# Another order of the steps within a slot on VectorE and ScalarE, in the mixing stage of a diffusion layer

## What is computed

```
o_rw  = (o_fwd + o_bwd), group norm per head of 64 channels, * ln_w + ln_b, + bonus, * gate
o_gla = (o_fwd + o_bwd), RMS norm per head of 96 channels, * norm_w * silu(g)
o     = concatenate([o_lru, o_rw, o_gla]) @ w_out            # 1024 x 1024
x     = x + g1 * o
h     = rmsnorm(x, norm2_g) * (1 + sc2) + sh2
probs = softmax(h @ w_router)                                # 16 experts
```

## Time and profile before

| | |
|---|---|
| median of 3 executions | 3443.15 us (3442.53 to 3450.62) |
| profiled execution, its own time | 3448.97 us |
| profiled execution, span | 3447.2 us |
| TensorE busy | 3111.8 us, 90% of the span |
| VectorE busy | 2279.6 us, 66% |
| ScalarE busy | 1609.5 us, 47% |
| GpSimd busy | 878.8 us, 25% |
| mixing stage, from the start of the first `rw_centre` to that of the last `keep_probs` | 1728.08 to 2044.66 us |

### The profile page before, as it was taken

One profiled execution on the slowest core, in us unless ns is written; L12 is line 12 of the kernel. 1 busy time (PEld: TensorE's weight loads), 2 busy tenths in 40 slices (PEclk: granted clock), 3 DMA queues, 4 the chain that ended last, 5 costly groups with the idle time before them and its releaser, 6 DMA issues. The chain is left out here.

```text
span 3447.2 us, 90906 instructions
## 1 busy us (share of the span) xinstructions
PE 3111.8 (90%) x37105; PEld 2856.9 (83%) x37105; DVE 2279.6 (66%) x4490; ACT 1609.5 (47%) x2917; POOL 878.8 (25%) x1232
## 2 busy tenths in 40 slices
PE   7899989999689999999869961999999999999996
PEld 4887867767489999999857740999999999999996
DVE  5565549995478888888777758555555555555555
ACT  3313656665445545554456530444444444444454
POOL 0110000000066667676422201012111111111113
PEclk8999989999899999999989975999999999999998
DMA  6455336665644554444276632556656556556685
GB/s 203 139 163 170 94 88 203 201 198 152 186 122 108 131 151 111 110 109 109 56 209 186 177 125 76 165 186 196 208 186 195 186 185 194 185 184 190 206 286 187
DMA packets 583428, 561.43 MB, mean 163 GB/s; under 512 B 211550, under 2 KB 527262, under 8 KB 582138
## 3 DMA queue, kind: packets, MB, share of 16 engines
q1 hardware_dynamic: 546652, 446.02, 43.2%
q0 software_dynamic: 36016, 109.52, 10.8%
q10 hardware_dynamic: 432, 1.25, 0.1%
HBM read 418.33 MB, written 138.33 MB: 161 GB/s over the span
## 5 line engine op out<-in xcount | busy, mean ns | idle before, releaser
L3456 DVE TENSOR_TENSOR exp_wlo<-exp_raw,exp_whi 128x2048 fp32r<-128x2048 f32 x192 | 439.9, 2292 | 366.3 <-ACT exp_whi L3357 354.4
L3357 ACT CAST exp_whi<-exp_raw 128x2048 fp32r<-128x2048 f32 x189 | 360.0, 1905 | 76.8 <-DMA exp_raw<-in_w_up 74.2
L1042 PE MATMUL mix_acc<-proj_hThi,mix_wlo 128*128 128x448 f32 (+3 forms) x920 | 357.6, 389 | 14.4 <-DVE mix_wlo L1410 14.4
L1042 PE MATMUL mix_acc<-proj_hTlo,mix_whi 128*128 128x448 f32 (+3 forms) x920 | 335.6, 365 | 0.0
L1042 PE MATMUL mix_acc<-proj_hThi,mix_whi 128*128 128x448 f32 (+3 forms) x920 | 335.4, 365 | 0.0
L3286 PE MATMUL moe_o<-moe_hidhi,exp_wlo 128*128 128x272 f32 x1024 | 307.5, 300 | 2.6 <-DVE moe_hidlo L3570 2.6
L3286 PE MATMUL moe_g<-moe_xThi,exp_wlo 128*128 128x272 f32 x1024 | 300.1, 293 | 1.0 <-DVE moe_xTlo L3460 1.0
L3286 PE MATMUL moe_o<-moe_hidhi,exp_whi 128*128 128x272 f32 x1024 | 297.8, 291 | 0.0
L3286 PE MATMUL moe_g<-moe_xThi,exp_whi 128*128 128x272 f32 x1024 | 297.3, 290 | 0.0
L3286 PE MATMUL moe_u<-moe_xThi,exp_wlo 128*128 128x272 f32 x1024 | 296.7, 290 | 0.0
L3286 PE MATMUL moe_u<-moe_xThi,exp_whi 128*128 128x272 f32 x1024 | 296.4, 289 | 0.0
(11 more groups left out here) (395 smaller groups left out, 8539.5 us busy)
## 6 DMA issues: line engine op xcount, KB each, us to landing
exp_raw<-in_w_gate SPq DMA_DIRECT2D x64, 1024.0 KB, 5.0
exp_raw<-in_w_up SPq DMA_DIRECT2D x64, 1024.0 KB, 5.1
exp_raw<-in_w_down SPq DMA_DIRECT2D x64, 1024.0 KB, 6.7
scn_plain<-rec SPq DMA_DIRECT2D x68, 384.0 KB, 3.8
rec<-mix_arena SPq DMA_DIRECT2D x24, 896.0 KB, 4.4
proj<-mix_out POOLq DMA_DIRECT2D x88, 224.0 KB, 2.5
scn_grc<-grec SPq DMA_DIRECT2D x136, 128.0 KB, 3.9
mix_arena<-in_w_ada SPq DMA_DIRECT2D x12, 1024.0 KB, 5.8
```

The lines of the kernel that those rows point to most:

```text
L1042: mm = pe.matmul(acc[n % ACCS][0:width, 0:tn], wt[:, k, 0:width], hT[hp][:, k, t0:t0 + tn], start=k == 0 and i == 0, stop=k == KD - 1 and ...
L3357: act.copy(w[k % RING][0][:, :, :], raw[k % RAW][:, :, :]).then_inc(hi_done[k % RING], 1)
L3456: dve.tensor_tensor(w[k % RING][1][:, :, :], raw[k % RAW][:, :, :], w[k % RING][0][:, :, :], ALU.subtract).then_inc(lo_done[k % RING], 1)
```

## The change

In the mixing stage the lists of steps of two engines are put in another order. No step is added, removed or altered, and no step moves to another slot or engine.

```
 @block.scalar
-each_slot((1, affine), (4, copy_h), (3, square), (0, rw_square), (5, exponential), (3, take_root), (0, gl_square), (0, roots), (1, high),
+each_slot((1, affine), (4, copy_h), (3, square), (0, rw_square), (5, exponential), (3, take_root), (0, gl_square), (1, high), (0, roots),
           (0, silu), (0, split_weights))

 @block.vector
-each_slot((4, copy_h), (3, residual), (5, top_logit), (0, rw_centre), (3, mean_square), (5, softmax), (3, norm), (0, variances),
-          (1, gated), (0, heads_normed), (1, low), (0, split_weights), (7, keep_probs))
+each_slot((3, residual), (4, copy_h), (5, top_logit), (0, rw_centre), (3, mean_square), (7, keep_probs), (1, gated), (5, softmax),
+          (3, norm), (0, variances), (1, low), (0, heads_normed), (0, split_weights))
```

## The result

The changed kernel takes 3408.78 us (median of 5, 3405.89 to 3413.45), the kernel before 3443.15 (median of 5, 3440.58 to 3450.62). The ratio is 0.990 with a 95% interval of 0.9886 to 0.9915, which is 29 to 39 us less. The forecast was 3413.4 in a range of 3406 to 3428.

A forecast was written before the change was run, and what follows sets the result against it. The prediction took VectorE's work plus its two waits for ScalarE to bound the mixing stage's slot. Savings of 22.6 us in twelve slots and 7.1 at the edges, 29.7 together, took 3443.15 to 3413.4 us, range 3406 to 3428.

The forecast's parts named there:

- What bounds the slot: Mixing stage: the 16.79 us slot is VectorE's work plus its waits of 2.21 for Exp and 1.15 for the root.
- The main term: VectorE: `keep_probs` and `gated` run during the 2.21 us wait for Exp, saving 1.92 us per slot, new slot 14.87.
- `low` and `high`: `low` ahead of `heads_normed` on VectorE, `high` ahead of `roots` on ScalarE: cost 0; without the latter 1.5 us a slot.
- `residual` first: VectorE: `residual` ahead of `copy_h` gives 0 per slot, 0.6 us once at the start, 2.1 in slot 19.
- the 1.0 of slot 17: Slot 17: TensorE becomes the bound at 13.86 us against 14.81 from product to product, saving 1.0.
- The edges: Slots 3, 4, 17 and 19 and the first `residual`: 3.4, 0.6, 1.0 and 2.1, together 7.1 us saved.
- The bound "up to 15.0" for the clock: TensorE: with the share of lowered clock unchanged the slot is 14.9 to 15.0, up to 1.5 us over 12 slots.
- The sum: Whole mixing stage: 22.6 us from twelve slots plus 7.1 from its ends, 29.7 us saved.
- B: Rival: TensorE becomes the bound with its clock lowered in many slots, time 3418 to 3428 us; chance 0.12.
- D: Rival: something the rows don't name paces the slot at 16.8 us, time 3436 to 3443 us; chance 0.05.
- C: Rival: late `affine` or gates' loads hold `gated` and the ring, deciding from 5.7 us lateness; 3464 us at 8; chance 0.03.

The follow-up runs named there:

- two passes: Changed kernel with the product's pass for the low part of the activations left out (32 matmuls per slot, not 48): slot 14.80 us, stage 281.12 us.
- No fill: Changed kernel with `keep_probs` and `gated` put behind `norm`, the other new order kept: slot 16.70 us, ratio 0.9986 to the kernel before.
- `gated` early: Changed kernel with `gated` ahead of `rw_centre` instead of behind `mean_square`: slot 16.54 us, stage 316.46 us, no ratio taken.
- `copy_h` first: Changed kernel with `copy_h` ahead of `residual` again: slot 14.81 us, stage 295.22 us, ratio 0.9921 to the kernel before.
- fill only: Kernel before with only `keep_probs` and `gated` moved ahead of `softmax`: slot 15.17 us, ratio 0.9936 to the kernel before.
- `keep_probs` last: Changed kernel with `keep_probs` last in the slot again, `gated` alone ahead of `softmax`: slot 14.99 us, stage 292.01 us, no ratio taken.
- second profile: Changed kernel run once more without any edit: stage 288.98 us, slot 14.80 us, ratio 0.9902 to the kernel before.

## Why the prediction was right

*What bounds the slot.* VectorE's work plus its two waits: confirmed by the profile after and by the two passes, in which TensorE lost a third of its product without moving the slot.

*The main term.* The steps start where they were foretold, counted from `residual`: `gated` at 4.85 (4.9), `low` at 12.50 (12.5), `heads_normed` at 13.64 (13.6). Foretold were 1.92 us per slot and 14.87, measured 1.99 and 14.80. The missing 0.07 is in `heads_normed`: 1.24 from its start to the next step before, 1.16 now (1884.68 to 1885.84). The remaining wait is 0.31 for a foretold 0.29. "No fill" gives 1.90 of it back, "`gated` early" 1.74. From `residual` of slot 5 to that of slot 17 it takes 177.9 us instead of 201.1: 23.2 for a foretold 22.6. Slot 5 alone is 15.14; the others make up for it.

*`low` and `high`.* Cost 0, and 1.5 us a slot had `high` stayed behind `roots`: the run shows 1.51.

*`residual` first.* The step for the slot was right (14.81 without it). At the end of the stage 2.1 were foretold for it and 2.2 came. But the 1.0 of slot 17, which the text gives to TensorE as the new bound, needs `residual` first too: "`copy_h` first" and "fill only" keep 14.81 and 14.80 there. At the start it was sized too small: 0.6 in the text, 1.2 and 3.1 us in the run, measured against the two profiles of the changed kernel.

*The edges.* 7.1 were foretold and 7.6 came in the first profile: 3.4 up to `residual` of slot 5 for a foretold 4.0; in slot 17, product to product, 14.81 - 13.64 = 1.2 for 1.0 (1960.66 to 1974.30 after); from the last product to the last transpose 2.2 for 2.1; and 0.8 behind it, which was counted at nothing and belongs to the earlier `keep_probs`, as the run with `keep_probs` last shows. In the second profile the first of these terms is 5.3, so that it is known to 2 us only. The text gave each of slots 3 and 4 the 1.72 of `gated`. That step fails for slot 4. From `residual` of slot 4 to that of slot 5 it takes 14.81 us in the kernel before, 14.77 with the fill only, 14.56 without the fill but with `residual` first, and 12.85 with both: with the fill alone VectorE stands 1.47 us in `copy_h` for TensorE's transposes instead.

*TensorE.* Its work was set at 14.50 and is 14.29, so the margin is 0.51 and not 0.37. The bound "up to 15.0" for the clock did not come about: the granted clock was 1.00.

*The sum.* 29.7 us for the stage against 30.8 in the first profile and 32.5 in the second. Against the medians the prediction is 4.6 us too high; 1 us of it is the stage, the rest lies within the scatter of what is ahead of it. That the time came out this close is in part luck: the start of the stage alone differed by 8.0 us between the two profiles of the first pair.

*The rivals.* B fell with the two passes. D fell with the slot. C, `gated` held by `affine` or the gates' loads, did not occur: L2833 shows no wait in any full slot. How late its inputs could come was not tried, so the 5.7 us from which it would decide stay a figure worked out. The Trainium skill's warning in "SBUF — State Buffer", section "SBUF: two separate sides", on GpSimd's DMAs beside VectorE has no effect that shows here: VectorE is busy for 88% of the slots, the transfers to `out_gl_of` land 8.6 us after their issue at most (8.2 before), and in the full slots no step of VectorE or ScalarE waits for a DMA.

## What to carry to other kernels

In an in-order engine a wait is a place for work: look for steps whose inputs have been there for long and whose results nobody needs at once, and put them behind the step that starts the other engine's chain and ahead of the step that waits for its end. Put ahead of the start they bring nothing.

The size of the wait is the limit of what can be gained. Then ask of each moved step which step of another engine it waits for in its new place. The two that fill the wait needed no partner: moved alone they gave 1.62 of the 1.99 us per slot. `low`, put ahead of `heads_normed`, did: without the swap on ScalarE (`high` ahead of `roots`) the slot is 16.31, longer than the 15.17 of the fill alone. A swap that is done by half can cost most of what the rest brings.

When the stage is a small part of the kernel, judge by its own length in the profile. It repeated to 2 us, while the part ahead of it alone ended anywhere within 31 us over the chips used.

## What the runs showed of the hardware

TensorE's clock differed between the kernels, and mostly with how long TensorE stood idle. In the windows over the full slots it stood without work for 18.4 of 201 us in the kernel before, and the granted clock was 0.97. In the changed kernel it was 0.4 of 177 us, and 1.00. With two passes it was 23.8 of 170 us, and 0.85 (windows view, columns as in the earlier trace rows):

```profile
1790.00:1960.00 170.00, 146.17 (x731) 122.88 (x730) 150.02 (x342) 114.33 (x207) 41.64 (x57) 0.85 0.77 211
```

This agrees with the Trainium skill, "TensorE: Matmul & The Clock Gate", section "What's actually happening": activity releases the throttle. But the sum of the idle time does not order all kernels. With no fill it is 12.7 of 200 us, less than in the kernel before, and yet the clock is lower:

```profile
1798.39:1998.38 199.99, 187.34 (x949) 156.01 (x948) 156.01 (x359) 120.30 (x217) 41.55 (x57) 0.94 0.62 176
```

Idle time is taken by modelled ends here, and which gaps let the clock fall was not looked into. For the changed kernel the bound of up to 15.0 us per slot, kept with the share of low clock unchanged, was not needed.

The part ahead of the mixing stage, the same in all kernels, ended between 1717 and 1748 us, and was late in all four runs of the third chip (1735 to 1748). Its cause is open.
